# Two-layer hybrid trunk on one core: first weight units by pieces, spreads as transpositions, sums by bank, and other distances between the operands

## What is computed

```python
def swiglu(x, w_gate, w_up, w_down):
    a = jnp.einsum('bsd,df->bsf', x, w_gate)
    u = jnp.einsum('bsd,df->bsf', x, w_up)
    return jnp.einsum('bsf,fd->bsd', jax.nn.silu(a) * u, w_down)
...
for l in range(DEPTH):
    x = x + 0.5 * swiglu(rmsnorm(x, ffn1_norm[l]), ffn1_w_gate[l], ffn1_w_up[l], ffn1_w_down[l])
    x = x + hybrid_mixer(rmsnorm(x, mix_norm[l]), w_in[l], ...)
    x = x + 0.5 * swiglu(rmsnorm(x, ffn2_norm[l]), ffn2_w_gate[l], ffn2_w_up[l], ffn2_w_down[l])
return rmsnorm(x, final_norm)
```

## Time and profile before

| | |
|---|---|
| median of 3 runs | 956.38 us |
| the three runs | 951.17, 956.38, 962.64 us |
| the profiled execution, its own time | 962.13 us |
| its span, first to last instruction | 960.2 us |
| mean granted clock of PE | 0.995 |
| busy: PE, PEld, DVE, ACT, POOL | 948.2 (99%), 940.4 (98%), 613.1 (64%), 456.0 (47%), 2.8 us |
| DMA | 169.05 MB, mean 176 GB/s |

### The profile page before, as it was taken

How to read it: one execution, slowest core, us unless ns; L and a number is a source line. 1 busy time by engine, 2 the same in 40 slices (tenths; PEclk the granted TensorE clock), 3 DMA queues, 4 the chain that set the end, 5 groups by cost and what they waited for, 6 DMA issues and landing times.

```text
span 960.2 us, 19406 instructions
## 1 busy us (share of the span) xinstructions
PE 948.2 (99%) x8188; PEld 940.4 (98%) x8188; DVE 613.1 (64%) x732; ACT 456.0 (47%) x490; POOL 2.8 (0%) x6
## 2 busy tenths in 40 slices
PE   9999999999999999999999999999999999999996
PEld 9999999999999999999999999999999999999996
DVE  6756555587868655555696565657796775555653
ACT  7433443457646443344453434346584643344332
POOL 0000000000000000000000000000000000000001
PEclk9999999999999999999999999999999999999998
DMA  8665565554345665556556565655523675556521
GB/s 288 213 218 175 178 196 190 181 154 133 89 154 179 218 194 190 183 175 195 165 175 218 191 200 180 213 175 167 186 63 90 218 234 189 175 178 204 186 87 44
DMA packets 130613, 169.05 MB, mean 176 GB/s; under 512 B 3216, under 2 KB 116112, under 8 KB 130576
## 3 DMA queue, kind: packets, MB, share of 16 engines
q1 hardware_dynamic: 130576, 168.52, 54.9%
HBM read 167.46 MB, written 1.05 MB: 175 GB/s over the span
## 4 chain that ended last, share of the span: by engine, by line
PE 93%; DVE 3%; ACT 2%; DMA 0%; issue 0%; SPq 0%; DVEq 0%
PE ps L358 29%; PE ps L359 29%; PE ps L360 29%; PE ps L415 1%; PE ps L565 1%; PE ps L578 1%; DVE wlo L1023 1%; DMA raw<-in_ffn_w_gate 0%; DVE resid L1050 0%; PE ps L724 0%; ACT sq L814 0%; ACT whi L793 0%; PE ps L702 0%; DVE work L1293 0%; DVE xlo L1028 0%
## 5 line engine op out<-in xcount | busy, mean ns | idle before, releaser
L1023 DVE TENSOR_TENSOR wlo<-raw,whi 128x2048 fp32r<-128x2048 f32 (+1 forms) x159 | 355.8, 2238 | 254.8 <-ACT whi L793 254.8
L358 PE MATMUL ps<-xhi,whi 128*128 128x256 f32 x1680 | 471.3, 281 | 0.0
L360 PE MATMUL ps<-xhi,wlo 128*128 128x256 f32 x1680 | 468.9, 279 | 0.0
L359 PE MATMUL ps<-xlo,whi 128*128 128x256 f32 x1680 | 468.9, 279 | 0.0
L793 ACT ACTIVATE whi<-raw 128x2048 fp32r<-128x2048 f32 (+1 forms) x159 | 297.3, 1870 | 165.9 <-PE ps L360 160.9
L358 PEld LDWEIGHTS ps<-xhi,whi 128*128 128x128 f32 x1680 | 318.2, 189 | 1.7 <-issue 1.0
L360 PEld LDWEIGHTS ps<-xhi,wlo 128*128 128x128 f32 x1680 | 316.8, 189 | 0.0
L359 PEld LDWEIGHTS ps<-xlo,whi 128*128 128x128 f32 x1680 | 315.6, 188 | 0.0
L358 PE MATMUL ps<-h_parts,whi 128*128 128x256 f32 x768 | 215.1, 280 | 0.1
L359 PE MATMUL ps<-h_parts,whi 128*128 128x256 f32 x768 | 214.8, 280 | 0.0
L360 PE MATMUL ps<-h_parts,wlo 128*128 128x256 f32 x768 | 214.8, 280 | 0.0
(11 more groups left out here) (150 smaller groups left out, 486.8 us busy)
## 6 DMA issues: line engine op xcount, KB each, us to landing
raw<-in_ffn_w_down SPq DMA_DIRECT2D x44, 1024.0 KB, 4.9
raw<-in_ffn_w_up SPq DMA_DIRECT2D x43, 1024.0 KB, 5.4
raw<-in_ffn_w_gate SPq DMA_DIRECT2D x42, 1024.0 KB, 5.3
raw<-in_w_in SPq DMA_DIRECT2D x12, 1024.0 KB, 5.2
raw<-in_w_in SPq DMA_DIRECT2D x8, 512.0 KB, 4.9
raw<-in_w_out SPq DMA_DIRECT2D x8, 512.0 KB, 4.5
raw<-in_w_in SPq DMA_DIRECT2D x2, 1088.0 KB, 5.2
raw<-in_ffn_w_gate SPq DMA_DIRECT2D x8, 256.0 KB, 6.8
```

The lines of the kernel that those rows point to most:

```text
L358: pe.matmul(o, w_hi, x_hi, start=start, stop=False, skip_group_check=True)
L359: pe.matmul(o, w_hi, x_lo, start=False, stop=False, skip_group_check=True)
L360: return pe.matmul(o, w_lo, x_hi, start=False, stop=stop, skip_group_check=True)
L1023: nc.vector.tensor_tensor(lo, r, h.bitcast(F32), ALU.subtract).then_inc(lo_done, 1)
```

## The change

Six edits, in one diff (cut to its core; the two functions `keep_warm` and `first_group`, shown above, are removed, and semaphore counts follow the new order).

- *Start.* ACT's queue issues the norm's gains and the first two pieces of the first gate unit (QUEUED is 2); SP issues x and pieces of all three units in turn, and after them the fourth unit, the second up unit, in pieces too, each when the first unit's low piece is done. ACT and DVE do per piece the input, then three units, then squares and their sum. PE does `first_units`: piece by piece the high and low products of the three units, interleaved; `square_sums(0)` stands behind piece 2; after piece 3 comes the spread and then the fourth unit by pieces, whose subtractions on DVE lie around `norm_b` and `gate_out`. The warming products in between are gone; WARM is 16 instead of 14.
- *Spreads.* `spread` uses `pe.transpose` instead of a product.
- *GLA sums.* The 8 sums run in the order of heads 0, 2, 1, 3, and the first two wait only for the first bank's squares.
- *End.* The last pair of tiles of the residual and its squares go tile by tile; the sums over partitions go by tile with the sum over the first four tiles last, and the scaled output is made in another order.
- *Distances.* `gap_x` is 64 instead of 96 columns of 4 bytes and `gap_h` 80 instead of 32: `xhi` and `xlo` lie 320 bytes from the weights modulo 512, `h_parts` 256.

```diff
+QUEUED = 2
...
-WARM = 14
+WARM = 16
...
-        sb("gap_x", [P, 96])
+        sb("gap_x", [P, 64])
...
-        sb("gap_h", [P, 32])
+        sb("gap_h", [P, 80])
...
+        def first_piece(q, u, p):
+            w, c = ((fg[0], 0), (fu[0], 0), (fg[0], UC), (fu[0], UC))[u]
+            q.dma_start(raw[:, u % 3, 2 * p * UC:(2 * p + 2) * UC].rearrange("p (k c) -> p k c", k=2),
+                        w[0, 2 * p * P:(2 * p + 2) * P, c:c + UC].rearrange("(k p) c -> p k c", p=P)
+                        ).then_inc(s_piece[u][p], 16)
...
+            for p in range(PIECES):
+                two = slice(2 * p, 2 * p + 2)
+                sp.dma_start(resid[:, two, :], xt[:, two, :]).then_inc(s_x[p], 16)
+                if p >= QUEUED:
+                    first_piece(sp, 0, p)
+                first_piece(sp, 1, p)
+                first_piece(sp, 2, p)
+            sp.dma_start(cst[:, :], cst_d).then_inc(s_cst, 16)
+            for p in range(PIECES):
+                if p < PIECES - 1:
+                    sp.wait_ge(lo_piece, 3 * p + 1)
+                else:
+                    sp.wait_ge(lo_done, 1)
+                sp.sem_inc(waits_met, 1)
+                first_piece(sp, 3, p)
             for l in range(DEPTH):
                 t0 = l * TURNS
-                load(0, t0 + 1, up_unit(fu[0], l, 1), SLOT, by_k)
+                if l:
+                    load(0, t0 + 1, up_unit(fu[0], l, 1), SLOT, by_k)
...
-                    last = pe.matmul(o[i // 4][:, i % 4 * P:(i % 4 + 1) * P], y[:, i:i + 1].to_broadcast([P, P]), ident,
-                                     start=True, stop=True, skip_group_check=True)
+                    last = pe.transpose(o[i // 4][:, i % 4 * P:(i % 4 + 1) * P], y[:, i:i + 1].to_broadcast([P, P]), ident)
...
+            def piece_hi(u, p, bank):
+                if p < PIECES - 1:
+                    pe.wait_ge(hi_piece, 3 * p + u + 1)
+                else:
+                    pe.wait_ge(hi_done, u + 1)
+                for k in (2 * p, 2 * p + 1):
+                    for ft in range(FT):
+                        pe.matmul(tiles(bank)[:, ft, :], weights(u, k, UC, ft * P, P)[0], xhi[:, k, :],
+                                  start=k == 0 and ft == 0, stop=False, skip_group_check=True)
+            def piece_lo(u, p, bank):
+                for k in (2 * p, 2 * p + 1):
+                    pe.wait_ge(xlo_done, k + 1)
+                    for ft in range(FT):
+                        pe.matmul(tiles(bank)[:, ft, :], weights(u, k, UC, ft * P, P)[0], xlo[:, k, :],
+                                  start=False, stop=False, skip_group_check=True)
+                if p < PIECES - 1:
+                    pe.wait_ge(lo_piece, 3 * p + u + 1)
+                else:
+                    split_ready(u, 0)
+                for k in (2 * p, 2 * p + 1):
+                    for ft in range(FT):
+                        last = pe.matmul(tiles(bank)[:, ft, :], weights(u, k, UC, ft * P, P)[1], xhi[:, k, :],
+                                         start=False, stop=k == KT - 1, skip_group_check=True)
+                if p == PIECES - 1:
+                    last.then_inc(unit_done, 1)
+            def first_units():
+                for p in range(PIECES):
+                    piece_hi(0, p, 2)
+                    if p == 0:
+                        piece_hi(1, p, 7)
+                    piece_lo(0, p, 2)
+                    if p:
+                        piece_hi(1, p, 7)
+                    piece_hi(2, p, 0)
+                    piece_lo(1, p, 7)
+                    piece_lo(2, p, 0)
+                    if p == PIECES - 2:
+                        square_sums(0)
+                pe.wait_ge(s_cst, 16)
+                spread_r(0, rs_y)
...
-                    square_sums(0)
-                    first_pieces(2, 0)
-                    spread_r(0, rs_y)
+                    first_units()
                 else:
                     split_ready(2, t)
                     up_tile(tiles(0)[:, 0, :], 2, 0)
                     spread_r(5 * l + 4 * f, rs_y)
                     up_tile(tiles(0)[:, 1, :], 2, 1).then_inc(unit_done, 1)
-                up(0, t + 1, 1)
+                    up(0, t + 1, 1)
...
-                    pe.wait_ge(osq_done, 2 * ev)
-                    for h in range(GH):
+                    for h in (0, 2, 1, 3):
+                        if h < 2:
+                            pe.wait_ge(osq_done, 2 * l + h + 1)
...
+            def column_sums(squares, first=False, last=False):
                 for t in range(TT):
-                    for m in (2 * p, 2 * p + 1):
-                        last = pe.matmul(ps[3][:, t:t + 1], sq[:, m, t * P:(t + 1) * P], ones[:, 0:1],
-                                         start=m == 2 and t == 0, stop=m == KT - 1, skip_group_check=True)
+                    done = pe.matmul(ps[3][:, t:t + 1], squares[:, t * P:(t + 1) * P], ones[:, 0:1],
+                                     start=first and t == 0, stop=last, skip_group_check=True)
+                return done
+            for m in range(4, KT):
+                pe.wait_ge(sq_done, 2 * (3 * DEPTH - 1) + (3 if m < 6 else m - 2))
+                column_sums(sq[:, m, :], first=m == 4)
+            pe.wait_ge(sqsum_done, 3 * DEPTH + 2)
+            last = column_sums(sqsum[:, :], last=True)
...
+            act.dma_start(gain0[:, :], gain0_d).then_inc(s_gain0, 16)
+            for p in range(QUEUED):
+                first_piece(act, 0, p)
...
-                first_hi(0, p)
-            for u in (1, 2):
-                for p in range(PIECES):
+                for u in range(3):
                     first_hi(u, p)
-                if u == 1:
-                    squares()
+                two = slice(2 * p, 2 * p + 2)
+                nc.scalar.activation(sq[:, two, :], resid[:, two, :], ACT.Square).then_inc(first_sq, 1)
+            for p in range(PIECES):
+                first_hi(3, p)
...
+            def scaled(m):
+                nc.scalar.activation(work[:, m, :], resid[:, m, :], ACT.Copy,
+                                     scale=par[:, G_NEXT + m:G_NEXT + m + 1]).then_inc(scaled_done, 1)
+            for p in range(KT // 2 - 1):
                 act.wait_ge(resid_up, 4 * v + p + 1)
                 nc.scalar.activation(sq[:, 2 * p:2 * p + 2, :], resid[:, 2 * p:2 * p + 2, :],
                                      ACT.Square).then_inc(sq_done, 1)
-            for m in range(KT):
-                nc.scalar.activation(work[:, m, :], resid[:, m, :], ACT.Copy,
-                                     scale=par[:, G_NEXT + m:G_NEXT + m + 1]).then_inc(scaled_done, 1)
+                if p < 2:
+                    scaled(2 * p)
+                    scaled(2 * p + 1)
+            for m in (KT - 2, KT - 1):
+                act.wait_ge(resid_up, 4 * v + m - 2)
+                nc.scalar.activation(sq[:, m, :], resid[:, m, :], ACT.Square).then_inc(sq_done, 1)
+            for m in range(4, KT):
+                scaled(m)
...
+                    if p == 3 and gain is None:
+                        for m in range(2):
+                            x = resid[:, KT - 2 + m, :]
+                            nc.vector.scalar_tensor_tensor(out=x, in0=acc[p][:, m, :], scalar=scale, in1=x,
+                                                           op0=ALU.mult, op1=ALU.add).then_inc(resid_up, 1)
+                        continue
...
+                if l or f:
+                    split_lo(0, t + 1)
+                else:
+                    for p in range(2):
+                        first_lo(3, p)
                 norm_b(v)
                 dve.wait_ge(rb_done, v + 1)
                 gate_out(grp, 3 * t, 2)
+                if not (l or f):
+                    for p in range(2, PIECES):
+                        first_lo(3, p)
                 up_out(grp, 3 * t + 1, 7)
...
-                first_lo(0, p)
+                for u in range(3):
+                    first_lo(u, p)
+                if p:
+                    dve.wait_ge(first_sq, p + 1)
+                    if p > 1:
+                        dve.wait_ge(sum_step, p - 1)
+                    nc.vector.tensor_tensor(flat(0, 2), flat(0, 2), flat(2 * p, 2 * p + 2), ALU.add
+                                            ).then_inc(sum_step, 1)
+            dve.wait_ge(sum_step, 3)
+            nc.vector.tensor_tensor(sqsum[:, :], sq[:, 0, :], sq[:, 1, :], ALU.add).then_inc(sqsum_done, 1)
             dve.sem_inc(resid_up, KT // 2)
-            for u in (1, 2):
-                for p in range(PIECES):
-                    first_lo(u, p)
-                if u == 1:
-                    sum_squares(0, 0)
...
+            dve.wait_ge(sqsum_done, 3 * DEPTH + 1)
+            nc.vector.tensor_tensor(sqsum[:, :], sq[:, 2, :], sq[:, 3, :], ALU.add).then_inc(sqsum_done, 1)
```

(39 more changed lines are left out.)

72 lines of the change are left out of this document (10 added, 62 removed).

## The result

| | before | after |
|---|---|---|
| median | 957.6 us (951.2, 956.4, 958.8, 962.6) | 970.9 us (970.8, 970.9, 970.9, 971.0) |
| ratio, 95% interval | | 1.014 (1.008 to 1.021) |
| span of the profiled execution | 960.2 us | 969.1 us |
| PE busy, instructions | 948.2 us, 8188 | 956.9 us, 8126 |

The changed kernel leaves 62 fewer records on PE and keeps PE busy for 8.7 us more. Two things stand out before any trace is opened. The time got worse by 1.4% (no change lies outside the interval; whether the loss reaches 2% stays open), and the spread of the runs went from 11.5 us to 0.2 us.

What follows compares the result with a forecast made beforehand. PE, busy with a chain of matmuls, was taken as the bound. From the profiled 962.1 us, terms of 6.6 gave 955.5; 5.7 less for levels of the median run gave 949.8, likeliest case 943 to 957, range 935 to 963.

Steps and rivals of the forecast that it cites:

- I take no systematic effect, levels as in the median run: Large matmuls: new distances change nothing systematically; two feed-forward stages slow, 5.7 us below the profile.
- a stretch at another spacing than these two (the distances act): Sign of being wrong: a long feed-forward stretch at a spacing other than 113 or 118 ns.
- 320 and 256 are unseen: Large matmuls: a distance can cost, but the new ones have no record; bounds 21 us saved to 11 us lost.
- the distances cost: Rival, large matmuls: 320 or 256 makes every one slow, adding 11 us, 966.5 us; chance 0.14.
- Levels picked by the start of the stream: Feed-forward stages: how the stream starts, not the old distance, decides between 113.3 and 117.8 ns; about 6.7 us a stage.
- more stages turn fast: Rival, second feed-forward stages: new spreads leave them fast, 6.7 us each, 942.1 us, or 935 with the first; chance 0.33.
- spreads inside the program: Mixers, second feed-forward parts, layer 1's first spread and GLA: transpositions need fewer records, saving 1.5 + 1.8 us.
- last spread: End, at granted clock 0.50: two records instead of four, saving 0.4 us.
- GLA sums: GLA sums of both layers: the wait for the last square and its issue gap go, saving 0.9 us in all.
- start: Start up to the first down unit: h_lo ends at 32.6 instead of 34.23 us, saving 1.7 us.
- other edits at the end: Final sums: fewer records follow the last square, some running ahead, saving 0.3 us, between 0 and 0.5.
- the stall of 1.1 us: Start, ahead of piece 3: PE waits 1.1 us for DVE's work on that piece, until 20.5 us.

Runs made afterwards that it cites:

- all_112: The changed kernel with xhi, xlo and h_parts at 112 bytes from the weights modulo 256; 935.7 us median, ratio 0.978.
- before_transpose: The kernel before the change, its own gaps kept, with only the spreads as transpositions; 941.4 us median, ratio 0.985.
- old_gaps_products: The changed kernel with the old distances (448 and 192) and the spreads as products again; 953.9 us median, ratio 0.999.
- before_112: The kernel before the change with only its operands moved to 112 bytes from the weights modulo 256; 945.29 us median.
- before_h_256: The kernel before the change with gap_h 48 instead of 32, so only h_parts moves, from 192 to 256 bytes; 958.9 us, one run.

## Why the prediction was wrong

**The step that failed is "I take no systematic effect, levels as in the median run".** The distances do have one, on every large matmul. Summed from start to start, `xhi` and `xlo` take 603.7 us in the changed kernel and 582.5 in `all_112`, `h_parts` 277.0 and 261.7, everything else 80.8 and 82.0: 35.3 us, where the medians differ by 35.2. The prediction had 934.5 us with every large matmul at 113.3 (955.5 - 21) and 15.3 more at the levels that it took (949.8). With the level held fast the measurement is 935.7, and 35.2 come on top. Of the miss of 21.1 us, 19.9 are what the distances cost beyond the levels it took, and 1.2 the rest. Its own sign of being wrong, "a stretch at another spacing than these two (the distances act)", is what the first view showed: 118.4 on average in the stretch from 40 to 200 us, 120.0 in every unit of `h_parts`.

**The rows had it.** M_V0, weights 64 bytes from `xhi`, ran at 117.8 in both layers, where the stages at 448 and 192 showed either level. The prediction read this as "320 and 256 are unseen". With the distance taken modulo 256, 320 is 64, and the trace had shown its price twice. Nobody could know the period from one trace; but "once fast, once slow at the one distance, always slow at the other" was a reason to give the slower rival more than 0.14. The changed kernel closes the circle: its M_V0 lies at 192 now, and starts 113.3 ns apart in both layers.

**The rival "the distances cost"** named the mechanism and the side. Its price was too low, 11 us: it put every large matmul at 117.8, and `h_parts` went to a level that before never shows, 120.0. The sentence beside it, that a third level would go past 970, is what happened: 970.9.

**The rule of the Trainium skill** (TensorE: Matmul & The Clock Gate, Part 2, the step LDWEIGHTS), that a weight load takes nothing from the running matmul, forecast no effect of the distances. The trace does not agree: one instruction stream at one clock runs at 113.3 to 123.3 ns, by nothing but the distance of the two operands in SBUF. That the two reads meet somewhere is the obvious reading, since only addresses differ, but it is argued and not shown; where they meet no run here shows.

**Levels picked by the start of the stream: right, and undervalued.** `before_transpose` and `old_gaps_products` show that the spreads turn it: at 192, as products, they turned the second feed-forward stage of both layers from fast to slow (113.4 ahead of the spread, 117.8 behind it), as transpositions they did not. That it "turns on a few ns" was not tested. The rival "more stages turn fast" (942.1, or 935 with all four) is what the change does at the old distances: 939.9 and 936.1. It had a chance of 0.33 and a doubt: "the distances change as well". The doubt was the case.

**The terms of the sum**, measured at 112, `before_112` against `all_112`:

| term | predicted | measured |
|---|---|---|
| spreads inside the program | 1.5 + 1.8 | 1.6 + 1.9 (3.49 at the sums of the end) |
| last spread | 0.4 | 0.6 |
| GLA sums | 0.9 | 0.6 in each layer, 1.2, without the clock's fall |
| start | 1.7 | 1.9 |
| other edits at the end | 0.3 | 0.6 |
| together | 6.6 | 8.0 (0.2 of it between the rows above), and 1.6 of the clock |

The four mechanisms stood and nearly every term was a little small, 1.4 us in all. The worth of the levels was a little large: before's large matmuls took 864.9 us in its profile and 846.6 in `before_112`, 18.3 less, or 19.9 without the 1.6 of the clock's fall there, where the prediction had 21 for the stages and the mixers; and the rest of PE's stream took 1.4 more. That the sum with all matmuls fast, 934.5, lies only 1.2 from the 935.7 measured is so in part because these errors cancel.

**The start by its steps.** PE began at 8.75 and not at 7.1: ACT waited 3.46 us for the first piece and made the first `xhi` at 7.18. So PE came to the sums at 21.5 and not at 19.4, found them ready, and the stall of 1.1 us forecast at `square_sums(0)` is not in the list of waits. The spread came at 26.23 (forecast 25.0), `h_lo` of the first down unit ended at 33.30 (forecast 32.6), and PE waits 1.1 us there (1.8). The gain that does not arrive was seen rightly: what DVE does between the spread and the first down unit sets it.

## What to carry to other kernels

Where PE is busy all the time and its count per stretch differs between stages with the same instructions, look at how far the moving operand lies from the weights in SBUF, modulo 256 bytes: here that alone moved the time by 3.8% in either kernel (970.9 against 935.7 us, 981.6 against 945.3). Try some distances in a stream of the kernel's own matmuls before choosing one, behind more than one kind of break, for a distance can be fast only by luck: 192 was fast in 11 blocks of 32, 112 in all 32. Do this first; only with the level held could terms of 0.5 us be told from each other.

## What the runs showed of the hardware

- The spacing of fp32r matmuls of 256 columns with a weight load each is set by the distance modulo 256 bytes (shown for the multiples of 32 and for 112), in steps: 113.3, 116.7, 117.8, 118.7, 120.0, up to 123.3 ns. No block settled under 113.3.
- At some distances (192, and by single blocks 16, 80, 128 and 144) two spacings are stable, and the stream keeps the one it has fallen into for as long as nothing breaks it, over 1500 matmuls in a stage. In `before_h_256`, with units at 256 in between, those at 448 ran at 113.3 in all four stages, but for the matmuls next to a spread.
- The GLA sums, 16 records of one column in 1.9 us with a wait of 0.3 us ahead of them, were followed by 3.4 us at a granted clock of 0.5 in 4 of the 10 places where kernels of the old order have them, and in none of the 12 where the sums run by bank and do not wait. That the missing wait prevents it is likely, but was not tried by itself.
- The first piece arrived later with two queues issuing than with one: PE's first real product is at 8.75 us instead of 7.15, and at 8.7 to 9.0 in the other kernels with the new start, 6.6 to 7.1 in those with the old one. Which of the two, the second queue or the changed order on the first, is the cause stays open.
